# Three FFNs of a two-block transformer: 2048 of 2816 inner columns made tokens-stationary and transposed

## The reference

```python
D_MODEL, SEQ, D_FF = 1024, 256, 2816

def swiglu(h, w_gate, w_up, w_down):
    return (jax.nn.silu(h @ w_gate) * (h @ w_up)) @ w_down

# in each of the two layers, with gains g:
h = swiglu(rms_norm(x, g[0]), w_gate[i, 0], w_up[i, 0], w_down[i, 0])
x = x + 0.5 * rms_norm(h, g[1])
...                                   # the mixer
h = swiglu(rms_norm(x, g[4]), w_gate[i, 1], w_up[i, 1], w_down[i, 1])
x = x + 0.5 * rms_norm(h, g[5])
```

## Time and profile before

| | |
|---|---|
| time, median of 3 runs | 2435.75 us (2433.02 to 2436.6) |
| the profiled execution | 2438.0 us, its span 2436.7 us |
| PE busy, matmuls | 2370.6 us, 97%, 13900 |
| weight loads of PE | 2033.7 us, 83% |
| DVE, ACT, POOL busy | 62%, 49%, 12% |
| mean granted TensorE clock | 0.992 |
| read from HBM | 408 MB, 168 GB/s |

### The profile page before, as it was taken

The page is one execution under the profiler, slowest core; times in us unless marked ns, Lnnn a source line. Parts: engine busy times, 40 slices in busy tenths (PEclk is TensorE's granted clock), DMA queues, the critical chain, the costliest instruction groups (busy, mean ns, idle before and its releaser), DMA issues.

```text
span 2436.7 us, 34298 instructions
## 1 busy us (share of the span) xinstructions
PE 2370.6 (97%) x13900; PEld 2033.7 (83%) x13900; DVE 1516.7 (62%) x2307; ACT 1188.5 (49%) x1782; POOL 285.0 (12%) x247
## 2 busy tenths in 40 slices
PE   9999999989999999999999999999999998999999
PEld 8987787779979977777898787887998877887987
DVE  6555556676555547666665677755665687656654
ACT  5444454354444445444544465554554455554543
POOL 1100010000000000000000121433100122333000
PEclk9999999999999999999999999999999999999999
DMA  8765545456666655544666554445566554445554
GB/s 236 201 198 170 165 120 142 127 173 177 187 193 179 183 186 183 164 139 152 185 182 213 178 173 141 122 132 164 179 192 208 181 167 127 124 140 164 179 185 147
DMA packets 263278, 411.66 MB, mean 169 GB/s; under 512 B 13770, under 2 KB 129370, under 8 KB 263120
## 3 DMA queue, kind: packets, MB, share of 16 engines
q1 hardware_dynamic: 256256, 389.59, 52.5%
q0 software_dynamic: 6432, 19.28, 3.1%
q10 hardware_dynamic: 432, 0.59, 0.1%
HBM read 408.31 MB, written 1.10 MB: 168 GB/s over the span
## 4 chain that ended last, share of the span: by engine, by line
PE 78%; DVE 14%; ACT 5%; issue 2%; POOL 1%; DMA 1%; ACTq 0%; DVEq 0%
PE banks L1807 14%; PE banks L1809 14%; PE banks L1808 14%; PE banks L1833 9%; PE banks L1834 9%; PE banks L1842 9%; DVE w_lo L2397 4%; ACT w_hi L2086 3%; PE banks L1896 1%; PE banks L1956 1%; PE banks L1909 1%; DVE probs L2592 1%; DVE mx_merged L3080 1%; ACT probs L2203 1%; PE banks L1871 1%
## 5 line engine op out<-in xcount | busy, mean ns | idle before, releaser
L2397 DVE TENSOR_TENSOR w_lo<-w_raw,w_hi 128x1024 fp32r<-128x1024 f32 x688 | 838.7, 1225 | 669.7 <-ACT w_hi L2086 667.4
L2086 ACT ACTIVATE w_hi<-w_raw 128x1024 fp32r<-128x1024 f32 (+2 forms) x744 | 777.9, 1049 | 584.9 <-PE banks L1809 418.7
L1807 PE MATMUL banks<-w_hi,xt_hi 128*128 128x512 f32 (+2 forms) x1120 | 461.3, 412 | 12.4 <-DVE xt_lo L2425 4.3
L1809 PE MATMUL banks<-w_hi,xt_lo 128*128 128x512 f32 (+2 forms) x1120 | 441.4, 394 | 0.0
L1808 PE MATMUL banks<-w_lo,xt_hi 128*128 128x512 f32 (+2 forms) x1120 | 440.9, 394 | 0.0
L1833 PE MATMUL banks<-xt_hi,w_hi 128*128 128x256 f32 x1728 | 427.6, 285 | 4.5 <-DVE w_lo L2397 2.9
L1834 PE MATMUL banks<-xt_hi,w_lo 128*128 128x256 f32 x1728 | 426.2, 283 | 0.0
L1833 PEld LDWEIGHTS banks<-xt_hi,w_hi 128*128 128x128 f32 x1728 | 327.4, 189 | 6.4 <-issue 3.2
L1834 PEld LDWEIGHTS banks<-xt_hi,w_lo 128*128 128x128 f32 x1728 | 328.2, 190 | 0.0
L1807 PEld LDWEIGHTS banks<-w_hi,xt_hi 128*128 128x128 f32 x1120 | 213.3, 190 | 62.2 <-DVE w_lo L2397 12.1
L1809 PEld LDWEIGHTS banks<-w_hi,xt_lo 128*128 128x128 f32 x1120 | 213.1, 190 | 48.5
(11 more groups left out here) (417 smaller groups left out, 2949.0 us busy)
## 6 DMA issues: line engine op xcount, KB each, us to landing
w_raw<-in_w_mlp SPq DMA_DIRECT2D x128, 512.0 KB, 3.7
w_raw<-in_w_in SPq DMA_DIRECT2D x104, 512.0 KB, 3.8
w_raw<-in_ffn_w_gate SPq DMA_DIRECT2D x88, 512.0 KB, 4.0
w_raw<-in_ffn_w_up SPq DMA_DIRECT2D x88, 512.0 KB, 4.3
w_raw<-in_ffn_w_down SPq DMA_DIRECT2D x88, 512.0 KB, 3.6
w_raw<-in_attn_w_in SPq DMA_DIRECT2D x72, 512.0 KB, 3.8
w_raw<-in_ret_w_in SPq DMA_DIRECT2D x64, 512.0 KB, 3.8
w_raw<-in_ret_w_out SPq DMA_DIRECT2D x16, 512.0 KB, 3.7
```

The costliest lines, as they stand in the source:

```text
L1807: pe.matmul(bank, xh, wh, start=(c == 0), stop=False)
L1809: mm = pe.matmul(bank, xl, wh, start=False, stop=(c == b.chunks - 1))
L2086: act.activation(k.w_hi[i % SPLIT][:, 0:m], k.raw[i % RAW][:, 0:m], ACT.Copy).then_inc(*ev.mark(k.w_hi_made, ("w_hi", i)))
L2397: dve.tensor_tensor(lo, raw, hi.bitcast(F32), ALU.subtract).then_inc(*ev.mark(k.w_lo_made, ("w_lo", i)))
```

## The change

In the three skewed FFNs, hidden columns 512 to 2559 are made like the first 512: four more blocks of 512 columns by "mm" for gate and for up, silu and product with tokens on the partitions, and eight transposes per block. Only the last 256 columns (unit 10) stay with "mm_whole". There are two buffers ffn_inner in turn. The transposes of block n - 1 are issued between the gate and the up of block n; those of block 4 behind the gate of unit 10. At the first block, the step "row_wide" now comes ahead of the silu and the product.

```diff
         if self.skewed:
-            yield from self.hidden_by_tokens(ws, ht)
-            units = range(BLOCK // SEQ, n_hidden // SEQ)
+            yield from self.hidden_by_tokens(ws, n_hidden, ht)
+            units = range(n_hidden // BLOCK * BLOCK // SEQ, n_hidden // SEQ)
...
-    def hidden_by_tokens(self, ws, ht):
+    def hidden_by_tokens(self, ws, n_hidden, ht):
 
         st = self.st
-        inner = self.put(f"ffn_inner{st}", 51, [P, HALVES, BLOCK])
-        gate, up = yield from self.pair_of_blocks(self.xt, (ws[0], 0), (ws[1], 0))
-        for half in range(HALVES):
-            self.step("inner", st, half, gate, up, inner[:, half, :])
-        self.step("row_wide", st, self.row_means)
-
-        def turns():
+        inner = [self.put(f"ffn_inner{st}{n}", 51 + 4 * n, [P, HALVES, BLOCK]) for n in range(2)]
+
+        def turns(n):
             for half in range(HALVES):
-                self.turn(lambda h, c: inner[:, h, c * P:(c + 1) * P], ht, half, [(c, c) for c in range(BLOCK // P)], [("inner", st, half)])
-
-        self.inner_turns = turns
+                self.turn(lambda h, c: inner[n % 2][:, h, c * P:(c + 1) * P], ht, half, [(BLOCK // P * n + c, c) for c in range(BLOCK // P)], [("inner", st, n, half)])
+
+        for n in range(n_hidden // BLOCK):
+            if n == 0:
+                gate, up = yield from self.pair_of_blocks(self.xt, (ws[0], 0), (ws[1], 0))
+                self.step("row_wide", st, self.row_means)
+            else:
+                gate = yield from self.block(self.xt, ws[0], D, n * BLOCK, BLOCK)
+                turns(n - 1)
+                up = yield from self.block(self.xt, ws[1], D, n * BLOCK, BLOCK)
+            for half in range(HALVES):
+                self.step("inner", st, n, half, gate, up, inner[n % 2][:, half, :])
+        self.inner_turns = lambda: turns(n_hidden // BLOCK - 1)
```

More of the change, by code:

```diff
@@ L2143, in act_program @@
         if what == "inner":
-            st, half, gate, _, dst = of
+            st, n, half, gate, _, dst = of
             bank = yield from banks.of("blk", gate.uid, half)
@@ L2148, in act_program @@
             act.activation(dst, bank, ACT.Silu, scale=k.row_scale[:, half:half + 1]).then_inc(
-                *ev.mark(k.act_done, ("inner_act", st, half), ("bank", "blk", gate.uid, half)))
+                *ev.mark(k.act_done, ("inner_act", st, n, half), ("bank", "blk", gate.uid, half)))
             give_bank("blk", gate.uid, half)
@@ L2527, in dve_program @@
         if what == "inner":
-            st, half, _, up, dst = of
+            st, n, half, _, up, dst = of
             bank = yield from banks.of("blk", up.uid, half)
             q.wait_ge(*(yield from ev.of("blk", up.uid, half)))
-            q.wait_ge(*(yield from ev.of("inner_act", st, half)))
-            dve.tensor_tensor(dst, bank, dst, ALU.mult).then_inc(*ev.mark(k.dve_done, ("inner", st, half), ("bank", "blk", up.uid, half)))
+            q.wait_ge(*(yield from ev.of("inner_act", st, n, half)))
+            dve.tensor_tensor(dst, bank, dst, ALU.mult).then_inc(*ev.mark(k.dve_done, ("inner", st, n, half), ("bank", "blk", up.uid, half)))
             give_bank("blk", up.uid, half)
```

## The result

The changed kernel takes 2442.06 us (median of nine runs, 2439.85 to 2444.43), the kernel before in the same set of runs 2437.7 us (nine runs, 2433.02 to 2439.52): **ratio 1.0024, 95% interval 1.0016 to 1.0032**, slower by some 6 us by the ratio and 4.4 us by the medians. Forecast were +2.9 us, "within 0.2%" as the likeliest case (0.78), and a range of 2434.5 to 2443.0. The time lies in the range and the sign is right, but the size was too small: the ratio stands beyond 0.2%, where "slower" had 0.18, though its interval reaches down to 1.0016. Times in this document are medians; of before_xt_32_big_0, one run of four that took 7539.29 us at a mean granted clock of 0.298 is left out.

A forecast was written before the change was run, and what follows sets the result against it. TensorE's own never-waiting stream was taken to bound the FFN stretches. Per block 0.88 - 0.64 = +0.24 us, over twelve blocks +2.9 us, from the median 2435.75 to 2438.6 us; range 2434.5 to 2443.0.

The forecast's parts named there:

- (a): Gate and up matmuls of each new block: 192 of 256 columns become 96 of 512, saving 0.64 us per block.
- (b): Eight added transposes per block, all on PE's path: 0.88 us per block, bounds 0.79 and 0.88.
- (c) to (g): VectorE and ScalarE work, banks, loads, first-block order, unit 10 and the rest: all hidden or unchanged, cost 0.
- (f): Order at the first block, row_wide ahead of silu and product: over 4 us left until their transposes, cost 0.
- the stall of w_lo: Rival in the new blocks: paired evacuations delay the weight split, 0.3 us per block, 2442.3 us in all; chance 0.07.
- The clock: Rival: each block's transposes drop the clock, 1.6 us a drop, 19 us in all, 2457.7 us; chance 0.02.
- The gap rule: Skill's gap of N / 2.4 + 2.5 ns for warm matmuls, weighed for each block: +0.2 us per block, same sign.
- sustained 131 ns: Skill's figure for 512-column matmuls: blocks would save most of their time; held contradicted by the trace's 0.2333 us.

The follow-up runs named there:

- before_xt_32_big_0: Kernel before, with transposed x 32 bytes past a multiple of 128 and the stage-tensor region moved up 96 bytes to a multiple of 128: 2404.30 us, ratio 0.9871.
- xt_at_32: Changed kernel with transposed x 64 bytes lower, 32 bytes past a multiple of 128: 2434.82 us, ratio to the kernel before 0.9988.
- xt_at_0: Changed kernel with transposed x moved to start at a multiple of 128 bytes: 2426.87 us, ratio to the kernel before 0.9957.
- few_turns: Changed kernel with two transposes per block of 512 columns instead of eight, evacuations kept at their length: FFN stretch 102.52 us instead of 105.80, run once.
- two_blocks: Changed kernel with only blocks 1 and 2 of the four in the new form, columns 1536 to 2815 left in units of 256: ratio 1.0009 to the kernel before.
- before_xt_32: Kernel before, with transposed x placed 32 bytes past a multiple of 128: 2424.15 us, ratio 0.9947 to the kernel before as given.
- before_xt_0: Kernel before, with transposed x placed at a multiple of 128 bytes: 2429.7 us, ratio 0.9968 to the kernel before as given.

## Why the prediction was right or wrong

**(a) Projections: the term that failed.** The saving was put at 0.64 us per block and is 23.04 - 22.49 = 0.55 us. The 23.04 and the count of matmuls hold. The price of 0.2333 us was taken from matmuls with hidden values as stationary operand, and the sentence that it may be taken at both ends, since the first block with x "is as free of waits", was the mistake: freedom from waits says nothing of the pace of the stream itself. The row for the same operand was in the trace, 0.2343, and xt_at_32 and xt_at_0 show that the difference is one of place. With it the sum is 12 x (0.88 - 0.55) = +4.0 us, against 3.8 in the trace; the 1.1 us that were missing are over a quarter of the result. The statement that halving the loads "gives back no more than 7 ns per pair" holds at the places measured at that time only: at 0 the pair costs 0.240 and the long one 0.227, 13 ns less; a block then saves 1.2 us, more than its transposes cost, and the change gains.

**(b) Transposes: right.** 0.88 us per block, on the path, 0.109 each (few_turns); per block, not per FFN (two_blocks).

**(c) to (g) Covers: right.** PE idle is 0.0 in these stretches, and no wait of PE for w_lo, a bank or ffn_inner is in the list of waits. The groups view of the changed kernel, 546.7 to 652.4 us, has them:

```profile
L1813 PE MATMUL banks<-w_hi,xt_hi 128*128 128x512 f32 x128 | 51.1, 400 | 0.0
...
L2403 DVE TENSOR_TENSOR w_lo<-w_raw,w_hi 128x1024 fp32r<-128x1024 f32 x36 | 44.1, 1226 | 49.2 <-ACT w_hi L2092 49.2
L2092 ACT ACTIVATE w_hi<-w_raw 128x1024 fp32r<-128x1024 f32 x36 | 38.2, 1060 | 54.1 <-PE banks L1815 51.6 <-PE banks L1848 2.5
```

VectorE, with 56.14 us instead of 63.06 in the first stretch, got lighter as said, and PE's idle time of 0.0 in both shows that this cost or gave nothing. The order at the first block, (f), is in all the changed kernels and left no wait, but wasn't tried alone.

**The sum against the median.** The working was made for 2438.0 and carried to a median of three runs, 2435.75; with nine runs the median of before is 2437.7, 27 in the next set gave 2437.2. Part of the distance between 2438.6 and 2442.06 is that. The forecast of "within 0.2%" had +2.9 us beside a bound of 4.9; with 4.0 the bound would have been 0.9 us away, less than the medians differ from set to set, and 0.18 for "slower" was too little. That the time lies in the range is in part luck: its upper end, 2443.0, was set by the stall of w_lo, which did not happen, and this made up for a base, read from three runs, that was some 2 us too low.

**The rivals.** The clock kept 1.00 through all fifteen groups of transposes, so the Trainium skill's statement in "TensorE: Matmul & The Clock Gate", section "Part 4: PE-mode transpose", that they don't count as PE-busy in the same way, changed nothing in this mix. Outside the FFNs the granted clock of the long stretches is the same within 0.01 in both kernels (0.98 in both ahead of the first FFN stretch). The gap rule of the same page, section "Back-to-back issue gap", gave +0.2 us per block; measured were +0.32. By that section's sustained 131 ns the blocks would have saved 10.5 of their 23.04 us (an estimate), under half and not "most of their time"; measured were 0.55. Both the gap rule and my rows of hidden values gave the right sign for the places as they were. Neither could have given it for xt at 0, where the sign is the other one.

## What to carry to other kernels

In a stream that never waits, price each matmul from a row with the same operands in the same roles, for a nanosecond times a thousand is the result. Where two forms come within a few per cent of each other, compare them at more than one address of the operands: here moving x by 96 bytes turned the sign of a change, and moving it by 64 and the stage tensors by 96 was worth 1.3% by itself, more than the choice of form tried here (0.2%).

## What the runs showed of the hardware that was not expected

- A 512-column fp32r matmul stands 0.2343, 0.2333 or 0.2268 to 0.2273 us behind the last at granted clock 1.00, by the start address of its stationary operand (96 bytes past a multiple of 128, 32 or 64 past one, or at one), with the same instructions in the same order.
- A 256-column one with x moving is quickest with x 32 bytes past (0.1167 us or, in another steady pace, 0.118), has 0.118 at 64, and 0.1200 at 0 and at 96; the weights were at multiples of 128 throughout. So the best place for an operand depends on its role.
- Two steady paces of the same stream, 2.80 and 2.83 us per tile, were seen in one execution. The pace changed where something had interrupted the stream: eight transposes in before_xt_32, a wait of 0.19 us for w_lo in the first FFN of before_xt_32_big_0. Why, and which bits of an address matter, is open; other places of w_hi and w_lo, and larger steps than 96 bytes, weren't tried.
- In two kernels with this stage and the place of xt alike, and another form of the FFNs ahead, the granted clock fell in one and not in the other. PE's weight loads waited 3.38 us for w_lo ahead of the retention's q and k columns in xt_at_0 and 2.68 us in before_xt_0; from 922 to 926 us the clock was then 0.50 (the level of 1.2 GHz) in the first and 1.00 in the second. It cost 2.7 us over the 154 steps.
